# Hierarchical scores of gated linear attention: few full-width score matmuls per level in place of many small-tile ones

## The reference, cut to what matters

```
# first block, 2 layers: 4 heads, key width 64 (chunk-causal, decay exp(-|b_i - b_j|))
decay = jnp.exp(-jnp.abs(b[:, :, None] - b[:, None, :]))
attn = jnp.einsum('bihd,bjhd,bijhd->bhij', qc, kc, decay)
o_intra = jnp.einsum('bhij,bjhv->bihv', attn, vc)
o_inter = jnp.einsum('bihd,bhdv->bihv', qc * jnp.exp(b), state)

# second block (hgrn2_mixer), 1 layer: 8 heads, key width 128 (causal)
diff = jnp.where(causal, b[:, :, :, None, :] - b[:, :, None, :, :], -jnp.inf)
scores = jnp.einsum('bhtsk,bhsk->bhts', qc[:, :, :, None, :] * jnp.exp(diff), kc)
```

## Time and profile before

| | us |
|---|---|
| median of 3 executions | 2258.02 |
| lowest and highest | 2256.87, 2259.39 |
| the profiled execution's own time | 2258.02 |
| its span, first to last instruction | 2256.2 |
| PE busy | 2241.8 (99%) |
| DVE busy | 1551.0 (69%) |
| ACT busy | 1298.2 (58%) |

### The profile page before, as it was taken

How to read it: one execution, slowest core, us unless ns; L and a number is a source line. 1 busy time by engine, 2 the same in 40 slices (tenths; PEclk the granted TensorE clock), 3 DMA queues, 4 the chain that set the end, 5 groups by cost and what they waited for, 6 DMA issues and landing times.

```text
span 2256.2 us, 35134 instructions
## 1 busy us (share of the span) xinstructions
PE 2241.8 (99%) x14045; PEld 2015.4 (89%) x14045; DVE 1551.0 (69%) x1757; ACT 1298.2 (58%) x1741; POOL 12.9 (1%) x18
## 2 busy tenths in 40 slices
PE   9999999999999999999999999999999999999998
PEld 8899998888999988889998999988999999998887
DVE  6576577775766777788786677866766766665555
ACT  6445576454555764666765467555655655554444
POOL 0000000000000000000000000000000000000000
PEclk9999999999999999999999999999999999999999
DMA  9655557676545684656566556685666666667664
GB/s 324 213 163 175 174 181 280 229 236 201 169 152 187 194 296 153 224 189 187 178 197 194 181 173 200 202 283 198 204 200 203 196 205 203 197 223 242 202 202 148
DMA packets 130548, 460.04 MB, mean 204 GB/s; under 512 B 13864, under 2 KB 20560, under 8 KB 128464
## 3 DMA queue, kind: packets, MB, share of 16 engines
q1 hardware_dynamic: 129392, 451.43, 61.1%
q0 software_dynamic: 848, 6.30, 0.8%
q10 hardware_dynamic: 144, 0.07, 0.0%
HBM read 449.35 MB, written 8.40 MB: 203 GB/s over the span
## 4 chain that ended last, share of the span: by engine, by line
PE 97%; DVE 1%; DMA 1%; ACT 1%; issue 0%; SPq 0%; DVEq 0%; ACTq 0%
PE banks L317 92%; PE banks L417 1%; PE banks L402 1%; PE banks L446 1%; PE banks L381 1%; PE banks L409 1%; DVE wl L650 0%; DMA w_bc<-in_norm_mix_post 0%; DMA early<-in_kv_t 0%; ACT wh L483 0%; PE banks L461 0%; PE banks L460 0%; PE banks L459 0%; PE banks L425 0%; DVE b L828 0%
## 5 line engine op out<-in xcount | busy, mean ns | idle before, releaser
L650 DVE TENSOR_TENSOR wl<-raw,wh 128x1024 fp32r<-128x1024 f32 x774 | 940.9, 1222 | 485.4 <-ACT wh L483 482.2
L483 ACT ACTIVATE wh<-raw 128x1024 fp32r<-128x1024 f32 (+1 forms) x777 | 814.3, 1053 | 506.4 <-PE banks L317 429.6
L317 PE MATMUL banks<-xx,wh 128*128 128x512 f32 (+1 forms) x3760 | 858.2, 380 | 0.0
L317 PEld LDWEIGHTS banks<-xx,wh 128*128 128x128 f32 (+1 forms) x3760 | 688.3, 189 | 91.9 <-issue 1.0
L317 PEld LDWEIGHTS banks<-xx,wl 128*128 128x128 f32 x3712 | 455.3, 192 | 13.7
L317 PE MATMUL banks<-xx,wl 128*128 128x256 f32 x3712 | 465.1, 276 | 0.0
L317 PE MATMUL banks<-wh,xx 128*128 128x512 f32 x1504 | 360.2, 380 | 0.0
L317 PEld LDWEIGHTS banks<-wh,xx 128*128 128x128 f32 x1504 | 282.7, 189 | 39.4
L317 PE MATMUL banks<-wl,xx 128*128 128x512 f32 x752 | 196.1, 379 | 0.0
L317 PEld LDWEIGHTS banks<-wl,xx 128*128 128x128 f32 x752 | 142.1, 189 | 20.2
L317 PE MATMUL banks<-wh,yy 128*128 128x512 f32 x416 | 98.4, 379 | 0.0
(11 more groups left out here) (280 smaller groups left out, 1757.3 us busy)
## 6 DMA issues: line engine op xcount, KB each, us to landing
raw<-in_w_in_f SPq DMA_DIRECT2D x304, 512.0 KB, 3.6
raw<-in_w_ffn_f SPq DMA_DIRECT2D x160, 512.0 KB, 4.0
raw<-in_w_ffn_down SPq DMA_DIRECT2D x88, 512.0 KB, 4.5
raw<-in_w_in_t SPq DMA_DIRECT2D x80, 512.0 KB, 3.7
raw<-in_w_out_t SPq DMA_DIRECT2D x64, 512.0 KB, 4.7
raw<-in_w_o_t SPq DMA_DIRECT2D x32, 512.0 KB, 4.7
raw<-in_kv_f SPq DMA_DIRECT2D x16, 512.0 KB, 3.9
raw<-in_w_up_a_f SPq DMA_DIRECT2D x16, 512.0 KB, 3.6
```

The lines of the kernel that those rows point to most:

```text
L317: return self.e.matmul(bank, stationary, moving, start=start, stop=stop, skip_group_check=True)
L483: self.e.activation(hi, source, ACT.Copy).then_inc(done.sem, 1)
L650: self.e.tensor_tensor(lo, source, hi.bitcast(f32), ALU.subtract).then_inc(done.sem, 1)
```

## The change

1. `level` loses its list of blocks. It now makes one matmul for each tile and head, with all 128 keys as stationary columns: 8 matmuls at each level. The moving operand is all 128 queries for `both` (at level 64: the last 66 of them), else the queries from position s-1 on in each stretch of 2s.
2. For the second block (`both` False) the levels 64 and 32 go to a new `level_of_blocks`, with the old block shapes; its loop over blocks g is now outside those over tiles and heads.
3. A new number `a.lone` (64 for `both`, else 16) is the level at which the last token's own score is made. There DVE copies the undecayed last query into a column that is otherwise unused, and the undecayed last key, so that the ordinary matmul of that level gives the score; the 8 extra matmuls (L449) go. `decay` at that level multiplies nearly all keys (127 of each 128).
4. `keep_awake` writes bank 7 alone.

```diff
-                keys = 64 if s == 64 or both and s == 32 else 32
-                blocks = (0,) if s == 64 else (0, 64) if s == 32 else (0, 32, 64, 96)
...
+                part = (lambda x: x) if both else (lambda x: from_last(x, s, s == a.lone))
                 for t in range(2):
                     for h in range(4):
                         r, c = a.heads(h)
                         c = c + t * P
                         i, n = a.where(h, t)
-                        for g in blocks:
-                            j = self.e.matmul(met(banks[6 + i][g:g + keys, n * P:(n + 1) * P], g), lk[r, c + g:c + g + keys],
-                                              met(rq[r, c:c + P], g), start=True, stop=True)
-                        if s == 16:
-                            j = self.e.matmul(banks[6 + i][96:P, n * P + 62:n * P + 63], a.k[r, c + 96:c + P],
-                                              a.q[r, c + P - 1:c + P], start=True, stop=True)
+                        j = self.e.matmul(part(banks[6 + i][:, n * P:(n + 1) * P]), lk[r, c:c + P], part(rq[r, c:c + P]),
+                                          start=True, stop=True)
+                j.then_inc(done.sem, 1)
+
+            def level_of_blocks(self, a, s, made, free, done):
+
+                self.wait_ge(*made, *free)
+                for g in range(0, P, 2 * s):
+                    for t in range(2):
+                        for h in range(4):
+                            c = a.heads(h)[1] + t * P
+                            i, n = a.where(h, t)
+                            j = self.e.matmul(banks[6 + i][g:g + s, n * P + g + s - 1:n * P + g + 2 * s], a.ke[:, c + g:c + g + s],
+                                              a.qe[:, c + g + s - 1:c + g + 2 * s], start=True, stop=True)
                 j.then_inc(done.sem, 1)
...
+                elif s == a.lone:
+                    left = lambda x: x.rearrange("p (g s) -> p g s", s=P)[:, :, 0:P - 1]
+                    lone = a.qe.rearrange("p (g b s) -> p g b s", b=P // (2 * s), s=2 * s)[:, :, :, s - 2:s - 1]
+                    last = every(a.q, P - 1).rearrange("p g (b o) -> p g b o", b=1)
+                    self.e.tensor_copy(lone, last.to_broadcast([P, a.tiles * 2, P // (2 * s), 1]))
+                    self.e.tensor_copy(every(a.ke, P - 1), every(a.k, P - 1))
+                    self.e.tensor_tensor(from_last(a.qe, s), from_last(a.q, s), from_last(a.ee, s), ALU.mult).then_inc(done[0].sem, 1)
+                    self.e.tensor_tensor(left(a.ke), left(a.k), left(a.ee), ALU.mult).then_inc(done[1].sem, 1)
...
-                    if s == 16:
-                        self.e.tensor_tensor(a.ke, a.k, a.ee, ALU.mult).then_inc(done[1].sem, 1)
-                    elif s > 1:
+                    if s > 1:
...
-                    if s == 16:
+                    if s == a.lone:
                         alone = after(merged_scores)
                         x.merge_last_token(a, tok, before, alone)
```

More of the change, by code:

```diff
@@ L121, in halves, with from_last @@
     return v[:, :, 0:s], v[:, :, s:2 * s]
-def from_last(x, s):
-    return x.rearrange("p (g s) -> p g s", s=2 * s)[:, :, s - 1:2 * s]
+def from_last(x, s, more=0):
+    return x.rearrange("p (g s) -> p g s", s=2 * s)[:, :, s - 1 - more:2 * s]
 def every(x, first):
@@ L184 @@
         forget_exps = forget_gates = forget_sum = gate_by = gate_half = gate_sum = gate_y = hi_features = \
[L185 to L192, removed]
+        inverse_root = join = keep_awake = last_rows = level = level_of_blocks = linear_values = \
+        lo_features = load = load_tables = load_vec = make_hi = make_lo = maxima = mean_squares = \
+        merge_last_token = merge_level = merge_sums = moments = narrow = narrow_sum = negate = norm = \
+        normalize = post_root = products_of_weights = project_gates = read_scores = rms_factor = root_means = \
+        scale_and_shift = scale_out = scale_value = scores = shift_keys = shift_z = soft_parts = \
+        soft_parts_of_row = split_act = split_squares = spread_factors = square = standard_scores = store = \
+        store_rows = store_scratch = sum_squares = take_outputs = turn = turn_softmax = unit_f = unit_t = \
+        values = weigh_features = weigh_post = weigh_z = nothing
 def build(nc, A, out):
@@ L311, in keep_awake @@
                 self.wait_ge(*waits)
-                for k in range(n):
-                    self.e.matmul(banks[bank + k % 2], tile, tile.rearrange("p (o c) -> p o c", o=1).to_broadcast([P, 4, P]),
+                for _ in range(n):
+                    self.e.matmul(banks[bank], tile, tile.rearrange("p (o c) -> p o c", o=1).to_broadcast([P, 4, P]),
                                   start=True, stop=True)
@@ L802, in merge_last_token @@
                 self.wait_ge(made, before)
-                self.e.copy_predicated(every(a.acc[:, 0:1024], P - 1), mask, every(pairs[3][:, :], 62)).then_inc(done.sem, 1)
+                self.e.copy_predicated(every(a.acc[:, 0:1024], P - 1), mask, every(pairs[3][:, :], P - a.lone - 2)).then_inc(done.sem, 1)
             def split_squares(self, a, made, hi_done, lo_done):
@@ L993, in __init__ @@
                 self.hi, self.lo = hi[:, 0:1024], lo[:, 0:1024]
+                self.lone = 64 if both else 16
         def walk(x):
@@ L1464, in linear_attention @@
                     tok = after(leveled)
-                    x.level(a, s, both, a.ke if both or s > 1 else a.k, a.qe, d, bank_free[6] + bank_free[7], tok)
+                    if a.lone < s:
+                        x.level_of_blocks(a, s, d, bank_free[6] + bank_free[7], tok)
+                    else:
+                        x.level(a, s, both, a.ke if both or s > 1 else a.k, a.qe, d, bank_free[6] + bank_free[7], tok)
                     qe_free = (tok,)
                     yield
-                    if s == 16:
+                    if s == a.lone:
                         alone = after(merged_scores)
@@ L1566, in walk @@
             x.clear_asleep(asleep[:, :].bitcast(f32), cleared)
-            x.keep_awake(asleep[:, :], 6, 11, (cleared,))
+            x.keep_awake(asleep[:, :], 7, 11, (cleared,))
             x.load_tables()
```

## The result

The changed kernel takes 2272.04 us (2271.87 to 2272.14, 4 runs); the kernel before takes 2258.67 us in the same comparison (2256.87 to 2259.39, 4 runs). The ratio is 1.0061, 95% interval 1.0048 to 1.0075: slower by 0.6%, 13.4 us by the medians. The forecast was 2273.0, by 15.0 us more. The four executions of the kernel before spread over 2.5 us; in the next comparison 14 of them have a median of 2257.78, and the changed kernel is 14.3 us above that. The profiled executions stand at 2258.02 and 2273.14, their spans at 2256.2 and 2271.3, 15.1 us apart.

A forecast was written before the change was run, and what follows sets the result against it. The prediction took PE's instruction stream as the bound. It summed 5.7 (first block), 8.3 (second block's full-width levels) and 1.0 (its level 32) to +15.0 us, 2273.0 us on the median, 0.66% slower, range 2266.5 to 2276.5.

The forecast's parts named there:

- What bounds the kernel: Whole kernel: PE busy 2241.8 of 2256.2 us, waiting for keys only 2.8, so added PE time is added at the end.
- The price of a level in the stream: Score levels on PE: a small-tile group costs its row's own time plus 0.12 us; full-width groups lose nothing ahead.
- rival D: Second block's first call: five longer levels each pass 0.9 us on through DVE's queue, +4.2 us, 2277.2; chance 0.04.
- First block, +5.7: Two layers, seven levels each at 1.29 us, 9.03 against 6.18 before: +2.85 us a layer, +5.7 in all.
- Second block, +8.3: Two calls, levels 16 to 1 at 1.79 us each, 8.95 against 4.79 before: +4.16 a call, +8.3 us in all.
- the upper bound: Second block's full-width levels: 0.112 us a record whatever the moving columns, against 0.063 to 0.111 from below.
- Rival A: Full-width levels: moving columns set the pace, 6.24 for 8.95 us a second-block call; +8.6 us, 2266.6; chance 0.09.
- the pace is set by the stationary side: Score records on PE: pace proportional to stationary columns, 0.03 us for 32, about 0.06 for 64, 0.112 for 128.
- Level 32, +1.0: Second block: same matmuls, but key blocks no longer alternate, 1.31 us for 0.82, +0.49 a call, +1.0 in all.
- DVE and the start, 0: Longer keys' product and copies fit DVE's 2.1 us slack; `keep_awake` on one bank taken as 0, bounds 0 and +0.4.
- B: All 24 full-width levels: stationary side hidden, 0.054 us a record for 128 columns; -3.5 us, 2254.5; chance 0.02.
- C: Second block: PE's 2.8 us of waits for the keys vanish, so at most +12.2 us, 2270.2; chance 0.03.

The follow-up runs named there:

- Halves in a row: The changed kernel with the first block's matmuls reordered: heads 0 and 2 for both tiles, then heads 1 and 3; 2279.57 us.
- fewer stationary columns: The changed kernel with 32 instead of 128 stationary columns at the second block's levels 16 to 1, scores of keys 32 to 127 left out; 2269.71 us.
- the tuned kernel: The kernel before with 64-key blocks at the first block's levels 16 to 1, last-token matmuls moved to level 64, copies at the second block's level 16; 2264.26 us.
- other-order run: The kernel before, same small matmuls, with the loop over key blocks outermost at every level of the second block; 2270.35 us.

## Why the prediction was right, point by point

**What bounds the kernel.** Right: PE's busy time took 14.3 of the 15.1 us, and the waits for the keys stayed at 2.8.

**The price of a level in the stream.** The method (own time plus 0.12 for groups of small tiles, no edge ahead of full-width ones) gave every level of both kernels within 0.05 us where PE has its data in time. It falls short at three levels of the second block's first call. At levels 64 and 32 PE waits for the keys, and loses 0.08 us each beyond the wait and the price, before and after alike. Level 1 costs 2.06, not 1.79; there PE asks for the queries before DVE has them (L787 ends at 1074.58):

```profile
1073.36 1.22 DVE L787 TENSOR_TENSOR lqe<-q,le 128x1024 f32<-128x1024 f32 x1
```
```profile
1072.73 1.89 PE L317 MATMUL banks<-xx,wh 128*128 128x512 f32 x8
1074.63 2.05 PE L437 MATMUL banks<-lqe,k 128*128 128x128 f32 x16
```

Eight records worth 1.73 end the projection row's share at 1074.46, the group begins 0.17 later, and then its first interval is longer by another 0.10. Before, the same place lost 0.10. That is a trace of rival D: the loss there is 0.3 us, 0.2 of it new, where D asked for 4.2.

**First block, +5.7.** Measured +5.5 in the changed kernel and +5.6 by itself. Only level 64 was mis-sized, 1.24 for 1.29. Its pairs follow each other at 0.112 us like those of the other levels, as forecast; what is shorter is the step from the first pair to the second, 0.16 us for 0.21. Halves in a row confirmed that the pair on two halves is what makes it cheap.

**Second block, +8.3.** Measured +8.4 by the groups and +8.0 by the times; 0.2 of the 8.4 is the new loss at level 1 just named. I chose the upper bound, and the rows at 72 to 96 moving columns have it. Rival A is excluded for the changed kernel. But my sentence that the pace is set by the stationary side was too narrow. In the score rows of before the moving side was never more than one column longer than the stationary one, so they could not tell. With 32 stationary columns and 72 or more moving ones the moving side sets it, at the same rate a column. The sum was right because all full-width levels have 128 stationary columns and never more moving ones.

**Level 32, +1.0.** Measured +0.8: the level costs 1.23, not 1.31. Within a block the records do follow at 0.032, 0.029 and 0.035 in turn. What the sum lacked is that three records of the second block start beside records of the first, which saves some 0.09. The mechanism, lost overlap by the order of the loops, was right, as the order alone shows. All groups together cost 14.7 for the 15.0 of the sum.

**DVE and the start, 0.** DVE grew by 1.7 us in sum, and PE waited longer for it in two places alone, the 0.2 us at level 1 and the 0.3 us for `xl`. The first 11 matmuls kept their pace (4.33 us for 4.75, by the clock), and PE's waits for ACT behind them take the difference up.

**The rivals.** B would need half the measured pace. C did not occur. A's price for level 64 of the first block should read 0.39 + 8 x 0.057 = 0.85, not 0.80, which moves A from +8.6 to +8.7; nothing rests on it.

The overhead of some 60 cycles for each matmul that the Trainium skill gives (TensorEngine Tiling (Array Packing), Instruction Overhead), by an estimate 25 ns at 2.4 GHz, does not hold as the pace of these tiles. With neighbours, records start 9 ns apart (12 in the prediction, which took the row's own time with the last record's latency). Without neighbours they follow at 32 ns, but 32 stationary columns at 0.83 ns account for 27 of these, so no run here shows an overhead of this size by itself.

## What to carry to other kernels

Where TensorE is the bound, count a group of small matmuls by what it puts into the stream, from start to start: for each record the longer of its two sides, divided by how many tiles run side by side. Put matmuls of different column blocks and row halves next to each other in the order, keep one tile size within a group, and expect some 0.3 us for going into and out of small tiles (2.06 against 1.79 us at nearly the same pace, in the run with fewer stationary columns). Replacing many small float32 matmuls by few full ones loses when the small ones already overlap.

## What the runs showed of the hardware that was not expected

A change of tile size within a group costs about 0.17 us each time: (0.405 - 0.058)/2, from the 64- and 32-column records of the tuned kernel against the pairs of equal size.

Records on another half of the rows are started ahead of earlier ones in the program, as the run with halves in a row showed. Records in another column block are too. In the other-order run's level 32, of the last four heads, the 14th record to start begins 6 ns behind the 13th and lasts 0.217 us, as only the very first does (0.218; the others 0.193 to 0.198), though 16 records of the first block stand ahead of those of the second. Its levels of 64 records have the same at the 14th, 30th and 46th. In all these cases the record passes three others. That the longest record is the first on its tile is inferred.

The longer side of a float32 record counts at about 0.83 ns a column on either side. From start to start, 32, 64 and 128 stationary columns take 32, 58 and 112 ns, 5 more than the columns alone; over 32 stationary ones, 72, 80, 96 and 128 moving columns take 63, 69, 83 and 109 ns, 2 to 3 more. The Trainium skill (TensorE: Matmul & The Clock Gate, LDWEIGHTS) gives the time of the stationary part in ns as the number of columns divided by 1.2, by an estimate 107 ns for 128; the trace's 112 agrees, with 5 more.

In the tuned kernel the granted clock fell to 0.50 for 3.41 us at level 64 of each layer, which cost 3.3 us together, though PE's records left no gap there.
